# The second and third mixer of a three-layer fp32 network on one core: where the operands of the first output rows and the recurrence stand in the queues

## The chip, the cores and the metric

The kernel runs on one core of a Trainium2 chip. The core has TensorE (PE, the matrix engine, with its weight loads shown apart as PEld), VectorE (DVE), ScalarE (ACT), GpSimd (POOL) and SyncE (SP, here the queue that loads weights). Each engine works through its own queue in order, and the engines wait for one another on semaphores. The metric is the device time of the kernel in microseconds (us), the median of several runs. 0.2% of it is 1.9 us.

## What is computed

A sequence of 256 tokens (with 16 meta tokens ahead of it in the first layer) and a model width of 1024, all in fp32. A first layer with three kinds of mixing and a gated MLP, then two layers of which each has a mixer and a squared-ReLU MLP. The change touches only the mixers of these two layers:

```python
def mixer_ab(h, w_in, conv_w, ln_g, ln_b, w_out):        # "second mixer"
    u = h @ w_in
    u_val, u_gate, q, k, v = jnp.split(u, ...)
    ya = conformer_conv(u_val, u_gate, conv_w, ln_g, ln_b)   # GLU, 31 taps, layer norm, silu
    yb = moba_attention(q, k, v)                             # 8 heads of 64, causal, ALiBi
    return jnp.concatenate([ya, yb], axis=-1) @ w_out

def mixer_c(h, w_in, conv_w, conv_b, w_r, b_r, w_i, b_i, lam, w_out):   # "third mixer"
    gate, xr = jnp.split(h @ w_in, 2, axis=-1)
    xr = causal_depthwise_conv(xr, conv_w) + conv_b          # 4 taps
    r, i = sigmoid(xr @ w_r + b_r), sigmoid(xr @ w_i + b_i)
    a = exp(-8 * r * softplus(-lam))
    hseq = scan(a, sqrt(1 - a * a) * (i * xr))               # h_t = a_t h_{t-1} + b_t
    return (hseq * gelu(gate)) @ w_out
```

## The kernel before

**Weights and splitting.** All weights come as 275 slabs of 128x1024, in the order of use, through a ring of four buffers (`raw`, `whi`, `wlo`). To keep fp32 accuracy each slab is split in two parts: ACT copies it rounded to `whi` (L428), DVE subtracts to get `wlo` (L801). Activations are split in the same way, into `ahi` (ACT) and `alo` (DVE), or `hidhi` and `hidlo` for the hidden units of the MLPs. A product is then three matmuls, L1168 to L1170. `split_ahead(n)` splits slab n + 3 while slab n is used, since the buffer of slab n + 3 was that of slab n - 1.

**Columns and rows.** A "column" multiplies one slab of an input projection with all eight chunks of the activations, 24 matmuls, and DVE takes the result out of its bank with `take` (L843) into `proj`. Column i may start when `take` has emptied the bank of column i - 2. A "row" of an output projection multiplies chunk k of the mixed values with its slab into four banks that hold the whole output, again 24 matmuls. Its operand is prepared by `operand_hi` (ACT, L474) and then `operand_lo` (DVE, L817), both out of `af[:, k]`. Since `ahi` and `alo` hold the operand of the columns too, ACT waits for the last column (`slab_used`) before it writes the first row's part into `ahi`.

**What sets the order.** The order is written out by hand in each engine's program. In the second mixer one loop of slots u = 0 to 18 runs on every engine: attention of head pair s = u // 2 (scores, maxima, exponentials L495, normalizing L868, transposes, copies L517, values L1280), beside it the remaining columns (`IN2_STEP`, the last at u = 11), the parts of the convolution and its layer norm (L1055 multiplies by the inverse deviation), and the first rows (`OUT2_STEP`: row 0 at u = 13, row 1 at 14, row 2 at 16, row 3 at 17). `CAT2_STEP` says in which slot the operands of these rows are made: operand 0 at u = 12, operand 1 at 13.

**Third mixer.** Sixteen columns, first the eight of the recurrent branch (i = 0 to 7), then the eight of the gate branch (i = 8 to 15). Beside them DVE does the four taps (L1125), ACT the sigmoids and, at i = 10, eight exponentials (L757); POOL multiplies `y` by `af` (L397, eight) and squares the decay (L400, eight, each after its exponential); `decay_steps` (DVE, L1106, eight) multiplies (a² + 1) by a hyperbolic tangent, which gives a² - 1, in one instruction with both inputs in SBUF; ACT takes two square roots of four chunks each (L762); `recur(j)` multiplies (L1113) and scans (L1114); `gated_output(j)` multiplies by the GELU (L1137); then the operand is split and row j can run.

## Time and profile before

| | |
|---|---|
| runs | 954.03 us median of three (953.94 to 955.48) |
| profiled execution | 954.74 us, of it 953.0 us span |
| PE busy | 911.9 us (96% of the span) |
| DVE, ACT, POOL busy | 591.7, 464.6, 92.4 us |
| mean granted TensorE clock | 0.984 of full |

TensorE is busy nearly all the time, and the chain of work that ended last lies on it for 87% of the span. So a change of order can gain only where TensorE stands idle or runs at its lower clock. A line of a timeline gives start and length in us, engine and line, and in brackets how long the engine was idle before it and what ended the idle time.

### The profile page before, as it was taken

The numbers are of one execution on the slowest core, as the hardware profiler recorded it, in microseconds if no ns is written. First come the engines' busy times: TensorE is split into PE (matmuls) and PEld (weight loads), VectorE is DVE, ScalarE is ACT, GpSimd is POOL, SyncE is SP. The second block draws the span as 40 slices with busy tenths as digits, with TensorE's granted clock in tenths as the row PEclk, the third lists the DMA queues.
The fourth block names the chain that finished last, engine by engine and source line by source line (L and its number), as shares of the span: only waits on it lengthen the run. The fifth ranks groups of instructions, "written<-read, shape, count | busy, mean of one in ns | idle before, by whom it ended". The sixth has DMA issues, their size and how long they took to land.

```text
span 953.0 us, 19688 instructions
## 1 busy us (share of the span) xinstructions
PE 911.9 (96%) x7466; PEld 874.3 (92%) x7466; DVE 591.7 (62%) x962; ACT 464.6 (49%) x733; POOL 92.4 (10%) x153
## 2 busy tenths in 40 slices
PE   7999898999999999999899999999898999999996
PEld 7988688999999998977899999999898999999995
DVE  4666345666656576545476656666878865666555
ACT  5444455534444355433664444444777654444442
POOL 4110000200000004910010000000221100000001
PEclk8999799999999999999999999999999999999998
DMA  6433122655555653732435555555334455555541
GB/s 229 161 128 125 53 67 90 221 188 187 180 179 192 196 185 124 238 107 76 160 129 191 192 185 193 177 183 193 132 134 155 155 173 188 190 177 185 189 154 45
DMA packets 44079, 152.57 MB, mean 160 GB/s; under 512 B 5764, under 2 KB 6020, under 8 KB 44036
## 3 DMA queue, kind: packets, MB, share of 16 engines
q1 hardware_dynamic: 40752, 146.36, 46.5%
q0 software_dynamic: 2912, 5.48, 1.8%
q8 instruction: 30, 0.49, 0.2%
q10 hardware_dynamic: 372, 0.14, 0.1%
q14 instruction: 13, 0.11, 0.0%
HBM read 148.58 MB, written 1.05 MB: 157 GB/s over the span
## 4 chain that ended last, share of the span: by engine, by line
PE 87%; DVE 7%; ACT 4%; issue 1%; DMA 1%; SPq 0%; DVEq 0%; ACTq 0%
PE bank L1168 25%; PE bank L1170 25%; PE bank L1169 25%; DVE alo L824 2%; PE bank L1454 2%; PE bank L1381 2%; DVE h L834 1%; DVE wlo L801 1%; PE bank L1237 1%; ACT whi L428 1%; PE bank L1197 1%; PE bank L1536 1%; PE bank L1254 1%; DMA raw<-in_slabs 1%; PE bank L1190 1%
## 5 line engine op out<-in xcount | busy, mean ns | idle before, releaser
L1168 PE MATMUL bank<-ahi,whi 128*128 128x256 f32 (+1 forms) x1416 | 407.1, 288 | 11.0 <-DVE alo L817 5.8
L1170 PE MATMUL bank<-ahi,wlo 128*128 128x256 f32 (+1 forms) x1416 | 400.9, 283 | 0.0
L1169 PE MATMUL bank<-alo,whi 128*128 128x256 f32 (+1 forms) x1416 | 400.6, 283 | 0.0
L801 DVE TENSOR_TENSOR wlo<-raw,whi 128x1024 fp32r<-128x1024 f32 x275 | 336.5, 1232 | 40.7 <-ACT whi L428 40.4
L428 ACT ACTIVATE whi<-raw 128x1024 fp32r<-128x1024 f32 x275 | 284.5, 1051 | 129.6 <-PE bank L1170 119.0
L1168 PEld LDWEIGHTS bank<-ahi,whi 128*128 128x128 f32 x1416 | 269.7, 190 | 14.6 <-DVE alo L817 6.8
L1169 PEld LDWEIGHTS bank<-alo,whi 128*128 128x128 f32 x1416 | 269.7, 190 | 0.4
L1170 PEld LDWEIGHTS bank<-ahi,wlo 128*128 128x128 f32 x1416 | 269.9, 191 | 0.0
L1168 PE MATMUL bank<-hidhi,whi 128*128 128x256 f32 x688 | 192.8, 280 | 0.0
L1169 PE MATMUL bank<-hidlo,whi 128*128 128x256 f32 x688 | 192.5, 280 | 0.0
L1170 PE MATMUL bank<-hidhi,wlo 128*128 128x256 f32 x688 | 192.5, 280 | 0.0
L1169 PEld LDWEIGHTS bank<-hidlo,whi 128*128 128x128 f32 x688 | 129.5, 188 | 0.0
L1168 PEld LDWEIGHTS bank<-hidhi,whi 128*128 128x128 f32 x688 | 129.4, 188 | 0.0
L1170 PEld LDWEIGHTS bank<-hidhi,wlo 128*128 128x128 f32 x688 | 129.4, 188 | 0.0
L1067 DVE SCALAR_TENSOR_TENSOR hid<-bank,rstd 128x256 f32<-128x256 f32 x64 | 27.1, 424 | 126.5 <-PE bank L1170 124.4
L710 ACT ACTIVATE hidhi<-hid 128x256 fp32r<-128x256 f32 x64 | 26.9, 420 | 137.1 <-DVE hid L1067 133.9
L843 DVE SCALAR_TENSOR_TENSOR proj<-bank,rstd 128x256 f32<-128x256 f32 (+1 forms) x56 | 23.8, 427 | 61.1 <-PE bank L1170 58.8
L332 POOL TENSOR_TENSOR sq<-sq 128x256 f32<-128x256 f32 (+1 forms) x20 | 19.7, 1013 | 355.0 <-ACT sq L456 355.0
L621 ACT ACTIVATE hidhi<-hid 128x256 fp32r<-128x256 f32 x22 | 9.2, 418 | 61.9 <-DVE hid L991 61.9
L1190 PE MATMUL bank<-ahi,whi 128*128 128x256 f32 (+1 forms) x96 | 25.8, 306 | 8.4 <-ACT ahi L449 4.3
L387 POOL DMA_DIRECT2D shared<-zpad x64 | 31.4, 499 | 1.2 <-POOL zpad L382 1.2
L1074 DVE TENSOR_TENSOR hidlo<-hid,hidhi 128x256 fp32r<-128x256 f32 x64 | 27.2, 425 | 3.5 <-ACT hidhi L710 1.1
(183 smaller groups left out, 720.4 us busy)
## 6 DMA issues: line engine op xcount, KB each, us to landing
raw<-in_slabs SPq DMA_DIRECT2D x275, 512.0 KB, 3.4
shared<-zpad POOLq DMA_DIRECT2D x64, 35.5 KB, 3.1
shared<-in_convw POOLq DMA_DIRECT2D x4, 512.0 KB, 6.3
h<-in_xT SPq DMA_DIRECT2D x4, 272.0 KB, 4.0
vtok<-in_gatew POOLq DMA_DIRECT2D x2, 512.0 KB, 4.9
out<-y SPq DMA_DIRECT2D x4, 256.0 KB, 2.2
par<-in_par ACTq DMA_DIRECT2D x1, 72.0 KB, 3.2
poolw<-in_poolw ACTq DMA_DIRECT2D x1, 64.0 KB
```

Of the source, the lines that this page charges most:

```text
L332: pool.tensor_tensor(t8[:, j, :] if i == N_MIX0 else a, a, b, ALU.add).then_inc(sum_ready, 1)
L387: pool.dma_start(zsh[32 * s:32 * s + 32, k, g, :], zpad[32 * g:32 * g + 32, k, s:s + CONV_X])\
L428: act.activation(whi[:, n % R, :, :], raw[:, n % R, :, :], ACT.Copy).then_inc(hi_done, 1)
L710: act.activation(hidhi[:, f % 2, :], hid[:, f % 2, :], ACT.Square).then_inc(hid_hi, 1)
L801: dve.tensor_tensor(wlo[:, n % R, :, :], raw[:, n % R, :, :], whi[:, n % R, :, :].bitcast(F32), ALU.subtract).then_inc(lo_done, 1)
L843: dve.scalar_tensor_tensor(proj[:, d, lo:], src[:, lo:T1], scale, rstd[:, lo:], ALU.mult, ALU.mult).then_inc(gemm_evac, 1)
L1067: dve.scalar_tensor_tensor(hid[:, f % 2, :], col_bank(f)[:, NMETA:T1], 0.0, rstd[:, NMETA:], ALU.max, ALU.mult).then_inc(gemm_evac, 1)
L1074: dve.tensor_tensor(hidlo[:, f % 2, :], hid2[:, f % 2, :], hidhi[:, f % 2, :].bitcast(F32), ALU.subtract).then_inc(hid_lo, 1)
L1168: pe.matmul(dst, hi, xh, start=start, stop=False, skip_group_check=True)
L1169: pe.matmul(dst, hi, xl, start=False, stop=False, skip_group_check=True)
L1170: return pe.matmul(dst, lo, xh, start=False, stop=stop, skip_group_check=True)
L1190: pe.matmul(dst, w[:, slot, k, :], ahi[:, k, lo:], start=(k == 0 and w is whi), stop=False, skip_group_check=True)
```

## The change

In the second mixer (slots u):

- DVE: the layer norm's four multiplications (L1055) go ahead of the `take` of slot 11. Operand 0 follows this `take`, ahead of the slab split and of slot 12's maxima.
- ACT: the wait for the last column and `operand_hi` of operand 0 come first in slot 12, ahead of slot 12's probability copies and exponentials. The copy of the transposed values (`vtok`) stands ahead of the exponentials in slots 0, 4, 8 and 12, no longer behind them.
- PE: row 0 also waits for the `vtok` copy of the last head pair.

In the third mixer:

- The operands of rows 0 and 1 go to `hidhi` and `hidlo`, so ACT's wait for the last column moves from operand 0 to operand 2.
- `decay_steps` moves a column sooner: the first four stand between the `take` of i = 10 and its slab split, the others behind i = 11. The square roots, `recur(0)` and the GELUs move a column sooner too, and `recur(1)` now stands inside the column loop.
- Behind the columns, `operand_lo(j)` stands ahead of `gated_output(j + 1)`.

The diff:

```diff
@@ -279,6 +279,12 @@
...
+        def row_operand(s, k):
+
+            if s == A_LRU and k < 2:
+                return hidhi[:, k, :], hidlo[:, k, :]
+            return ahi[:, k, NMETA:], alo[:, k, NMETA:]
+
         def half(b, j):
@@ -471,7 +477,7 @@
...
                 act.wait_ge(af_ready, KC * f + k + 1)
-                act.activation(ahi[:, k, NMETA:], af[:, k, :], ACT.Copy).then_inc(ahi_ready, 1)
+                act.activation(row_operand(s, k)[0], af[:, k, :], ACT.Copy).then_inc(ahi_ready, 1)
@@ -652,22 +658,23 @@
...
                     n += 1
+                if u == max(IN2_STEP) + 1:
+                    act.wait_ge(slab_used, OUT2)
+                    operand_hi(A_CAT2, F_CAT2, CAT2_STEP[u])
                 if u % 2 == 0:
...
                         transposed(u // 2 - 1, FOX_S, moba_copies)
+                    if u % 4 == 0 and u < MOBA_U:
+                        pair = u // 4
+                        act.wait_ge(vT, 7 + pair)
+                        act.activation(vtok[:, 0:2, P * pair:P * pair + P],
+                                       acc_bank[2][:, 0:2 * P].rearrange("p (g d) -> p g d", g=2), ACT.Copy).then_inc(v_ready, 1)
                     if u // 2 < MOBA_S:
                         probabilities(u // 2, FOX_S, MOBA_N)
-                if u % 4 == 0 and u < MOBA_U:
-                    pair = u // 4
-                    act.wait_ge(vT, 7 + pair)
-                    act.activation(vtok[:, 0:2, P * pair:P * pair + P],
-                                   acc_bank[2][:, 0:2 * P].rearrange("p (g d) -> p g d", g=2), ACT.Copy).then_inc(v_ready, 1)
                 if u >= 6 and u % 4 == 2:
...
                     act.activation(af[:, PAIR_CHUNK[pair], :], aux_bank[:, 0:SEQ], ACT.Copy).then_inc(af_ready, 1)
-                if u == max(IN2_STEP) + 1:
-                    act.wait_ge(slab_used, OUT2)
                 if 2 <= u <= 2 * CONV_C and u % 2 == 0:
@@ -685,7 +692,7 @@
...
                             .then_inc(af_ready, 1)
-                if u in CAT2_STEP:
+                if u in CAT2_STEP and u > max(IN2_STEP) + 1:
                     operand_hi(A_CAT2, F_CAT2, CAT2_STEP[u])
@@ -756,19 +763,18 @@
...
                            .then_inc(lru_exp, 1)
-                if i in (12, 13):
-                    j = 4 * (i - 12)
+                if i in (11, 12):
+                    j = 4 * (i - 11)
                     act.wait_ge(lru_m2, j + 4)
...
                        .then_inc(lru_root, 4)
-                if i == 14:
-                    gelus(0, 3)
-            act.wait_ge(slab_used, OUT3)
+                if i in (13, 14):
+                    gelus(3 * (i - 13), 3 * (i - 12))
             for j in range(KC):
+                if j == 2:
+                    act.wait_ge(slab_used, OUT3)
                 operand_hi(A_LRU, F_LRU, j)
                 split_ahead(OUT3 + j - 1)
-                if j == 0:
-                    gelus(3, 6)
                 if j == 1:
@@ -814,8 +820,8 @@
...
                 dve.wait_ge(ahi_ready, KC * s + k + 1)
-                dve.tensor_tensor(alo[:, k, NMETA:], af[:, k, :], ahi[:, k, NMETA:].bitcast(F32), ALU.subtract)\
-                   .then_inc(alo_ready, 1)
+                hi, lo = row_operand(s, k)
+                dve.tensor_tensor(lo, af[:, k, :], hi.bitcast(F32), ALU.subtract).then_inc(alo_ready, 1)
@@ -1034,25 +1040,28 @@
...
+                if u == max(IN2_STEP) + 1:
+                    operand_lo(A_CAT2, CAT2_STEP[u])
+                    split_ahead(OUT2 - 1)
                 softmax_slot(u, MOBA_S, FOX_S, MOBA_N, alibi_bias)
+                if u == LN_VAR_STEP + 1:
+                    dve.wait_ge(ln_std, 1)
+                    for k in range(CONV_C):
+                        dve.tensor_tensor(cv[:, k, :], cv[:, k, :], r1[:, :], ALU.mult).then_inc(ln_norm, 1)
                 if u in IN2_STEP:
                     c = IN2_STEP[u]
-                    take(n, acc_bank[n % 2], c, QSCALE if 8 <= c < 12 else 1.0)
+                    take(n, acc_bank[n % 2], c, QSCALE if 8 <= c < 12 else 1.0, ahead=n < OUT2 - 1)
                     n += 1
...
                     n += 1
-                if u in CAT2_STEP:
+                if u in CAT2_STEP and u > max(IN2_STEP) + 1:
                     operand_lo(A_CAT2, CAT2_STEP[u])
...
                                                  ALU.mult, ALU.add).then_inc(ln_dev, 1)
-                if u == LN_VAR_STEP + 1:
-                    dve.wait_ge(ln_std, 1)
-                    for k in range(CONV_C):
-                        dve.tensor_tensor(cv[:, k, :], cv[:, k, :], r1[:, :], ALU.mult).then_inc(ln_norm, 1)
             for i in range(max(CAT2_STEP.values()) + 1, KC):
@@ -1114,7 +1123,10 @@
...
             for i, c in enumerate(IN3_ORDER):
-                take(IN3 + i, col_bank(i), c, ahead=IN3 + i < OUT3 - 1)
+                take(IN3 + i, col_bank(i), c, ahead=IN3 + i < OUT3 - 1 and i != 10)
+                if i == 10:
+                    decay_steps(range(4))
+                    split_ahead(IN3 + i)
                 if 1 <= i <= KC:
@@ -1127,20 +1139,19 @@
...
                     ins.then_inc(af_ready, 1)
-                if i in (11, 12):
-                    decay_steps(range(4 * (i - 11), 4 * (i - 10)))
-                if i == 13:
-                    recur(0)
+                if i == 11:
+                    decay_steps(range(4, KC))
+                if i in (12, 13):
+                    recur(i - 12)
...
             gated_output(0)
-            recur(1)
             for j in range(KC):
+                operand_lo(A_LRU, j)
                 if j + 1 < KC:
                     gated_output(j + 1)
-                operand_lo(A_LRU, j)
                 split_ahead(OUT3 + j - 1)
@@ -1210,7 +1221,7 @@
...
                 pe.wait_ge(alo_ready, KC * s + i + 1)
-                row(n0 + i, ahi[:, i, NMETA:], alo[:, i, NMETA:], first=(i == 0), last=(i == KC - 1))
+                row(n0 + i, *row_operand(s, i), first=(i == 0), last=(i == KC - 1))
@@ -1480,6 +1491,8 @@
...
                 if u in OUT2_STEP:
+                    if OUT2_STEP[u] == 0:
+                        pe.wait_ge(v_ready, 10)
                     operand_row(OUT2, A_CAT2, OUT2_STEP[u])
```

The changed kernel has the same number of instructions on each engine; in it a line number is 6 to 12 higher than before. First DVE's queue in the second mixer, slots 11 and 12: `proj` is the `take` of the last column, `t` the layer norm, `ssb` and `nmax` the maxima, `alo` operand 0. Before:

```order
L843 SCALAR_TENSOR_TENSOR proj<-bank,rstd 128x256 [waits slab_used]
L801 TENSOR_TENSOR wlo<-raw,whi 128x1024 [waits hi_done]
L1055 TENSOR_TENSOR t<-t,r 128x256 [waits ln_std]
L1055 TENSOR_TENSOR t<-t,r 128x256 x3
L1032 SCALAR_TENSOR_TENSOR ssb<-dist,bank 128x128 [waits p_ready,s_ready]
L1032 SCALAR_TENSOR_TENSOR ssb<-dist,bank 128x128 [waits p_ready]
L859 TENSOR_REDUCE nmax<-ssb 128x1 [waits s_biased] x2
L817 TENSOR_TENSOR alo<-af,ahi 128x256 [waits ahi_ready]
```

Now:

```order
L1050 TENSOR_TENSOR t<-t,r 128x256 [waits ln_std]
L1050 TENSOR_TENSOR t<-t,r 128x256 x3
L849 SCALAR_TENSOR_TENSOR proj<-bank,rstd 128x256 [waits slab_used]
L824 TENSOR_TENSOR alo<-af,ahi 128x256 [waits ahi_ready]
L807 TENSOR_TENSOR wlo<-raw,whi 128x1024 [waits hi_done]
L1038 SCALAR_TENSOR_TENSOR ssb<-dist,bank 128x128 [waits p_ready,s_ready]
L1038 SCALAR_TENSOR_TENSOR ssb<-dist,bank 128x128 [waits p_ready]
L865 TENSOR_REDUCE nmax<-ssb 128x1 [waits s_biased] x2
```

The layer norm went from behind the last `take` to ahead of it, and `alo` from behind the maxima to right behind the `take`, ahead of the slab split `wlo`.

ACT's queue at the same place, slot 12: `prob` are the exponentials, `probT` and `vtok` the copies out of the banks, `ahi` operand 0. Before:

```order
L428 ACTIVATE whi<-raw 128x1024 [waits slab_used,raw_loaded1]
L517 ACTIVATE probT<-bank 128x2x256 [waits o_ready,pT]
L495 ACTIVATE prob,rsum<-ssb,nmax 128x128 [waits pT,m_ready] x2
L663 ACTIVATE vtok<-bank 128x2x128 [waits vT]
L474 ACTIVATE ahi<-af 128x256 [waits af_ready,slab_used]
L428 ACTIVATE whi<-raw 128x1024 [waits slab_used,raw_loaded2]
```

Now:

```order
L434 ACTIVATE whi<-raw 128x1024 [waits slab_used,raw_loaded1]
L480 ACTIVATE ahi<-af 128x256 [waits af_ready,slab_used]
L523 ACTIVATE probT<-bank 128x2x256 [waits o_ready,pT]
L670 ACTIVATE vtok<-bank 128x2x128 [waits vT]
L501 ACTIVATE prob,rsum<-ssb,nmax 128x128 [waits pT,m_ready] x2
L434 ACTIVATE whi<-raw 128x1024 [waits slab_used,raw_loaded2]
```

`ahi`, with its wait for the last column, went from behind the exponentials to the head of the slot, and `vtok` ahead of the exponentials.

Last DVE's queue in the third mixer, from the `take` of i = 10 on: `sq<-sq,t` are the decay steps, `y` and `t` the two instructions of `recur`. Before:

```order
L843 SCALAR_TENSOR_TENSOR proj<-bank,rstd 128x256 [waits slab_used]
L801 TENSOR_TENSOR wlo<-raw,whi 128x1024 [waits hi_done]
L843 SCALAR_TENSOR_TENSOR proj<-bank,rstd 128x256 [waits slab_used]
L801 TENSOR_TENSOR wlo<-raw,whi 128x1024 [waits hi_done]
L1106 SCALAR_TENSOR_TENSOR sq<-sq,t 128x256 [waits lru_aa] x4
L843 SCALAR_TENSOR_TENSOR proj<-bank,rstd 128x256 [waits slab_used]
L801 TENSOR_TENSOR wlo<-raw,whi 128x1024 [waits hi_done]
L1106 SCALAR_TENSOR_TENSOR sq<-sq,t 128x256 [waits lru_aa] x4
L843 SCALAR_TENSOR_TENSOR proj<-bank,rstd 128x256 [waits slab_used]
L801 TENSOR_TENSOR wlo<-raw,whi 128x1024 [waits hi_done]
L1113 TENSOR_TENSOR y<-y,sq 128x256 [waits lru_ix,lru_root]
L1114 SCALAR_TENSOR_TENSOR t<-proj,y 128x256 [waits dve_chain]
```

Now:

```order
L849 SCALAR_TENSOR_TENSOR proj<-bank,rstd 128x256 [waits slab_used]
L1115 SCALAR_TENSOR_TENSOR sq<-sq,t 128x256 [waits lru_aa] x4
L807 TENSOR_TENSOR wlo<-raw,whi 128x1024 [waits hi_done]
L849 SCALAR_TENSOR_TENSOR proj<-bank,rstd 128x256 [waits slab_used]
L807 TENSOR_TENSOR wlo<-raw,whi 128x1024 [waits hi_done]
L1115 SCALAR_TENSOR_TENSOR sq<-sq,t 128x256 [waits lru_aa] x4
L849 SCALAR_TENSOR_TENSOR proj<-bank,rstd 128x256 [waits slab_used]
L807 TENSOR_TENSOR wlo<-raw,whi 128x1024 [waits hi_done]
L1122 TENSOR_TENSOR y<-y,sq 128x256 [waits lru_ix,lru_root]
L1123 SCALAR_TENSOR_TENSOR t<-proj,y 128x256 [waits dve_chain]
L849 SCALAR_TENSOR_TENSOR proj<-bank,rstd 128x256 [waits slab_used,dve_chain]
L807 TENSOR_TENSOR wlo<-raw,whi 128x1024 [waits hi_done]
```

The first four decay steps stand ahead of the split and of the next `take`, the second four ahead of the `take` of i = 12, and `recur(0)` ahead of the `take` of i = 13.

## Rows read from the trace of the kernel before

**Rows 1.** Waits of TensorE, 440 to 485: us in total, times, longest.

```profile
PE bank L1168 <- DVE alo L817: 4.7, 2, 3.2
```

**Rows 2.** Timeline of TensorE, second mixer: start us, us, instruction, idle before.

```profile
450.72 0.66 PE L1280 MATMUL bank<-probT,vtok 128*64 128x128 f32 x8 [0.47 <-ACT probT L517]
454.55 0.39 PE L1168 MATMUL bank<-ahi,whi 128*128 128x256 f32 x1 [3.17 <-DVE alo L817]
...
459.10 0.70 PE L1254 MATMUL bank<-proj 64*128 64x256 f32 x4
...
459.93 0.37 PE L1168 MATMUL bank<-ahi,whi 128*128 128x256 f32 x1
...
462.96 0.44 PE L1280 MATMUL bank<-probT,vtok 128*64 128x128 f32 x4
```

**Rows 3.** TensorE by stretches: window, length, busy, granted clock, DMA share, GB/s.

```profile
455.60:459.00 3.40, 3.40 (x18) 0.50 0.44 146
469.00:483.00 14.00, 14.00 (x115) 1.00 0.63 219
730.60:755.20 24.60, 24.52 (x192) 0.93 0.53 172
```

**Rows 4.** Timeline of DVE, second mixer.

```profile
449.07 0.42 DVE L843 SCALAR_TENSOR_TENSOR proj<-bank,rstd 128x256 f32<-128x256 f32 x1 [2.85 <-PE bank L1170]
449.41 1.22 DVE L801 TENSOR_TENSOR wlo<-raw,whi 128x1024 fp32r<-128x1024 f32 x1
450.54 1.42 DVE L1055 TENSOR_TENSOR t<-t,r 128x256 f32<-128x256 f32 x4
451.88 0.48 DVE L1032 SCALAR_TENSOR_TENSOR ssb<-dist,bank 128x128 f32<-128x128 f32 x2
...
454.07 0.43 DVE L817 TENSOR_TENSOR alo<-af,ahi 128x256 fp32r<-128x256 f32 x1 [1.32 <-ACT ahi L474]
```

**Rows 5.** Timeline of ACT, second mixer.

```profile
452.59 0.40 ACT L495 ACTIVATE prob<-ssb,nmax 128x128 f32<-128x128 f32 x1 [1.92 <-DVE nmax L859]
...
453.64 0.40 ACT L474 ACTIVATE ahi<-af 128x256 fp32r<-128x256 f32 x1
```

**Rows 6.** Timeline of TensorE, third mixer: column 14, then output row 0.

```profile
721.10 0.39 PE L1168 MATMUL bank<-ahi,whi 128*128 128x256 f32 x1 [0.21 <-DVE proj L843]
...
730.63 0.36 PE L1168 MATMUL bank<-ahi,whi 128*128 128x256 f32 x1 [3.65 <-issue]
```

**Rows 7.** Line L400 on POOL: duration ns min/median/max, first and last start.

```profile
L400 POOL TENSOR_TENSOR sq<-proj x8: 607/607/1592, 713.7 to 717.8; 128x256 f32<-128x256 f32 x8
```

**Rows 8.** Line L1125 on DVE, one in three beside POOL: the same columns.

```profile
L1125 DVE SCALAR_TENSOR_TENSOR af<-proj,par,af x24: 479/485/900, 680.7 to 707.9; 128x256 f32<-128x256 f32 x24
```

**Rows 9.** Timeline of DVE and POOL side by side, behind the third mixer.

```profile
757.26 4.70 DVE L824 SCALAR_TENSOR_TENSOR alo<-h,par,ahi 128x256 fp32r<-128x256 f32 x8
...
758.97 3.59 POOL L332 TENSOR_TENSOR sq<-sq 128x256 f32<-128x256 f32 x4 [39.54 <-ACT sq L456]
```

**Rows 10.** Timeline of DVE, third mixer.

```profile
722.10 1.42 DVE L1106 SCALAR_TENSOR_TENSOR sq<-sq,t 128x256 f32<-128x256 f32 x4
...
726.79 1.22 DVE L801 TENSOR_TENSOR wlo<-raw,whi 128x1024 fp32r<-128x1024 f32 x1
727.92 0.42 DVE L843 SCALAR_TENSOR_TENSOR proj<-bank,rstd 128x256 f32<-128x256 f32 x1
...
728.59 0.42 DVE L1113 TENSOR_TENSOR y<-y,sq 128x256 f32<-128x256 f32 x1
...
729.77 0.42 DVE L1137 TENSOR_TENSOR af<-t,proj 128x256 f32<-128x256 f32 x1
730.11 0.42 DVE L817 TENSOR_TENSOR alo<-af,ahi 128x256 fp32r<-128x256 f32 x1
```

**Rows 11.** Timeline of ACT, third mixer: a table load, and the first operand.

```profile
720.79 1.28 ACT L762 ACT_TABLE_LOAD   x1 [2.48 <-DVE sq L1106]
...
728.76 0.42 ACT L474 ACTIVATE ahi<-af 128x256 fp32r<-128x256 f32 x1 [0.62 <-DVE af L1137]
```

## The prediction

> **What bounds the kernel.** TensorE is busy for 96% of the span, so I first looked for where it waits, in the list of waits: in the second mixer it waits twice for an operand of an output row, 4.7 us together, the longer 3.2 [rows 1]. The timeline puts the longer one ahead of output row 0: the value products of slot 13 begin at 450.72 and last 0.66, then nothing until 454.55 [rows 2]. The granted clock then falls to 0.50 (1.2 GHz) from 455.6 to 459.0 [rows 3]; row 0 with what follows it takes 459.10 - 454.55 = 4.55, row 1 at full clock 462.96 - 459.93 = 3.03 [rows 2]. So the pause costs 3.17 and the fall 1.52. Behind the second wait, 4.7 - 3.17 = 1.5 long, the clock is 1.00 [rows 1, 3]. The third mixer has the same picture: TensorE stands for 3.65 ahead of row 0 (730.63) [rows 6], and the eight rows behind run at a mean clock of 0.93 over 24.6 us [rows 3], which costs 0.07 x 24.6 = 1.7. Together these are 3.17 + 1.52 + 3.65 + 1.7 = 10.0 us; the question is how much of them the new order can take away.
>
> **Second mixer.** Operand 0 is late because ACT makes it behind the exponentials (452.59), and these wait for the maxima, which DVE makes behind the split (449.41) and four layer norm multiplications (450.54 to 451.88) [rows 4, 5]. None of that is needed for it. Now: the last column is done at 449.07, when its `take` begins. ACT stands idle there and makes `ahi` in 0.40 [rows 5], done at 449.5; `take` needs 0.34 of DVE (449.07 to 449.41), then `alo` needs 0.43 [rows 4], done at 449.95. TensorE is still busy with its attention work until 450.72 + 0.66 = 451.38 [rows 2]. Row 0 also waits for the `vtok` copy, which is now behind the probability copy that releases the values at 450.72 [rows 2]; a copy of 0.4 as on line L474 [rows 5] ends at 451.1, hidden. So row 0 starts at 451.35 and the pause of 3.17 goes whole.
>
> What is late next? The multiplications fit into DVE's 2.85 of idle time ahead of the `take` (1.34 needed) [rows 4]. The split starts at 449.9 and the maxima at 449.9 + 1.13 = 451.0, against 451.88: 0.85 sooner. The exponentials are then at 451.75, and all that follows up to operand 1 moves with them: ACT's two exponentials 0.8, slab split 1.0, operand 0.4 give 453.8; DVE's slab split (1.13) starts at 453.5, operand 1 is ready at 455.05. TensorE comes to row 1 at 451.35 + 3.03 = 454.4, plus scores and transposes 0.83 (459.10 to 459.93) [rows 2] = 455.2. That is just enough. Row 1 starts 459.93 - 455.15 = 4.8 sooner if the clock no longer falls. Row 2 and the table load with the four Silu that cause the second wait follow TensorE's transposes and move by the same amount; that wait of 1.5 stays. The earlier `vtok` copies in slots 0, 4, 8 delay exponentials by 0.3 at most, ahead of a normalization that stands behind a column of TensorE: nothing. **Sum of the second mixer: -4.7**, with -3.1 if the clock falls all the same, and nothing beyond -4.8.
>
> **Third mixer.** Here I follow DVE, which decides. Before, the decay steps stood where POOL's squares were done. POOL makes the eight squares from 713.7 on, one each 0.58 ((717.8 - 713.7)/7), though the last took 1.59 [rows 7]. Now DVE comes to the first step after the `take` at 712.8 and has to wait for them, with the split of slab 13 and the `take` of column 11 queued behind it, on which TensorE's column 13 waits.
>
> And the two engines disturb one another. L1125, also an instruction with both inputs in SBUF, takes 0.48 alone and 0.90 where POOL multiplies beside it [rows 8]. Behind the third mixer POOL's four sums and L824 run in turns: four sums take 3.59, one each 0.87 = 0.57 + 0.30 [rows 9]. I take that turn for the decay steps. The Trainium skill, "SBUF — State Buffer", section "Who interferes with whom", says that a VectorE instruction with two SBUF inputs and a GpSimd instruction that reads SBUF exclude one another for a whole instruction. By that rule the decay steps beside POOL's squares run in turns, as the rows show for L1125 and L824; the case without it is a rival below.
>
> The steps, in us: square 0 is done at 714.3, but square 1 has begun, so step 0 runs behind it and is done at 715.1; steps 1 to 3 each 0.87 later, 717.7. A square goes first (718.3), then the split of slab 13: 719.4. `take` of column 11 done at 719.75. TensorE was ready for column 13 at 721.10 - 0.21 - 2.84 = 718.05 [rows 6] and starts at 719.8: a **new wait of 1.75**. DVE: split of slab 14, behind a square, 721.0; last square 721.6; four more steps 721.6 to 722.9 (1.42 alone, less the 0.08 by which an end overlaps the next start [rows 10]); `take` 12 done 723.25; column 14 could start at 722.65, starts at 723.3: wait 0.6. Then split 1.13, `recur(0)` 1.18 (728.59 to 729.77), `take` 0.34, split 1.13, `recur(1)` 1.18, `take` 0.34, split 1.13 [rows 10]: DVE reaches the last `take` at 729.55, column 15 was done at 728.95. `take` and `gated_output(0)` 0.67 (727.92 to 728.59) and 0.1 to finish: 730.3; ACT's `ahi` 0.42 [rows 11], hop, DVE's 0.42 [rows 10]: row 0 at **731.3**, against 730.63, after a wait of 2.35. ACT keeps up: its table load of 1.28 [rows 11] and roots begin at 717.8, and its last split is done at 728.1, DVE needs it at 728.4. The place in `hidhi` gains nothing by itself, since `gated_output(0)` still stands behind the last `take`.
>
> Behind it the order `operand_lo(j)`, `gated_output(j + 1)`, split, `recur` has the same sum as before, 0.34 + 0.34 + 1.13 + 1.18 = 3.0 for a row of 2.84. Operand 1 is ready 3.25 after operand 0, row 6 starts at 731.3 + 3.25 + 5 x 3.0 = 749.5, row 7 at 752.35, its end is 755.2: as before (755.15), if the clock stays up, because row 0 alone is later while the fall of 1.7 is spared. If it falls again (2.35 lies between 1.5 without and 3.17 with a fall [rows 1, 2]), DVE's slower pace hides a part: end 755.7. I take the middle. **Sum of the third mixer: +0.3** (0 to +0.6).
>
> **Total:** -4.7 + 0.3 = -4.4. The profiled execution took 954.74, which gives 950.3; the median of the runs is 0.7 lower, so the forecast is 954.03 - 4.4 = **949.6**.
>
> **Rivals.** (a) No turns between DVE and POOL: the four steps end at 716.4, slab 13 at 717.6, the `take` in time for 718.05; no new wait, row 0 at 728.9, rows paced by DVE end at 752.75 to 753.2, that is -2.1. Time 954.03 - 4.7 - 2.1 = 947.2. Against it speak rows 8 and 9; for it, that the decay step was never seen beside more than one square. (b) The clock falls in the second mixer all the same, since its attention work leaves TensorE short pauses (0.47 ahead of the values [rows 2]): 949.6 + 1.6 = 951.2. (c) Slower than before: POOL keeps the read path for all eight squares. At 0.87 each they end at 713.7 + 7.0 = 720.7, the four steps at 722.0, slab 13 at 723.2, column 13 starts at 723.6, 5.6 late. That pause is longer than both that brought a fall; against the forecast it costs 2.5 on DVE's path and two falls of 1.7 more, 5.9: 949.6 + 5.9 = 955.5. It decides from a start of column 13 some 3 us behind 719.8 on. (d) The moved operand does not release row 0, because another semaphore comes last (the slab, the bank of `vtok`): nothing is gained in the second mixer, 954.3. Against it: both lie ahead of 451.35 by the times above.
>
> **Numbers.** Forecast 0.62, (a) 0.15, (b) 0.15, (c) 0.03, (d) 0.05. The range takes in (a) and (b) with the spread of the runs: 946.8 to 951.9. 0.2% is 1.9 us, about what a measurement can tell: faster (below 952.1) 0.92, same 0.06, slower 0.02.
>
> **What would show it.** Second mixer: no wait of TensorE for `alo` ahead of row 0, clock 1.00 through rows 0 and 1, operand 1 within 0.2 of TensorE's arrival, and the wait ahead of row 3 still near 1.5. Third: squares and decay steps in turns at 0.87, a wait of 1.5 to 2 ahead of column 13, row 0 behind a pause of 2.3. I am wrong if column 13 starts without a wait (then 947), or if row 1 waits for its operand by more than 1 us.

## The result, and the profile after

The changed kernel takes **949.27 us** (median of 6 runs, 946.81 to 950.37); the kernel before took 955.01 beside it (6 runs, 953.94 to 955.48). The ratio is 0.9941, with a 95% interval of 0.9925 to 0.9957; the medians differ by 5.7 us. The forecast was 949.6, or 4.4 faster than the 954.03 shown with the kernel before.

The head of the profile's page after the change (busy time and instructions of each engine, then the granted clock in 40 slices, in tenths):

```profile
span 945.1 us, 19688 instructions
PE 907.3 (96%) x7466; PEld 869.1 (92%) x7466; DVE 593.4 (63%) x962; ACT 464.2 (49%) x733; POOL 93.7 (10%) x153
PEclk9999899999999999999999999999999999999998
```

The instruction counts are those of before. POOL is busy for 1.3 us more, though it does the same squares: a first sign of what the third mixer does now. TensorE's waits for output operands in the second mixer (440 to 480; us in total, times, longest):

```profile
PE bank L1179 <- DVE alo L824: 1.5, 1, 1.5
```

and in the third mixer (695 to 760), the first two rows:

```profile
PE bank L1179 <- issue: 2.1, 1, 2.1
PE bank L1179 <- DVE proj L849: 1.5, 2, 1.3
```

Of the two waits for `alo` in [rows 1], 4.7 together, the longer one is gone and the one of 1.5 stands. In the third mixer the pause ahead of row 0 has shrunk from 3.65 [rows 6] to 2.1 ("issue": the trace names nothing that ended the wait; DVE finishes operand 0 at 723.11, 0.1 ahead of row 0, so it is most likely the operand), and there is a new wait of 1.3 for the `take` of column 11, ahead of column 13. The wait of 0.2 ahead of column 14 was there before [rows 6]. The same stretches by engine (length, busy us of PE, PEld, DVE, ACT, POOL, the granted clock, DMA share, GB/s):

```profile
448.00:459.40 11.40, 11.38 (x96) 10.28 (x98) 8.11 (x20) 9.17 (x20) 0.00 (x0) 1.00 0.44 146
710.00:723.20 13.20, 9.60 (x77) 9.00 (x77) 12.58 (x21) 10.05 (x11) 3.49 (x3) 1.00 0.52 166
723.20:747.80 24.60, 23.88 (x192) 22.92 (x193) 22.77 (x39) 13.40 (x20) 0.00 (x0) 1.00 0.54 189
```

Through rows 0 to 2 of the second mixer TensorE works without a gap at full clock (11.38 of 11.40), where [rows 3] has a clock of 0.50 for 3.40 us. In the third mixer the clock also stays at 1.00, where [rows 3] has a mean of 0.93.

**Where the time went.** The profiled execution took 946.81, which is 7.9 less than the 954.74 of before. To divide this, I took the starts of the same matmuls in both traces and compared the lengths between them:

| stretch (time in the kernel before) | after less before, us | forecast |
|---|---|---|
| start to the first MLP (to 178.66) | -2.67 | 0 |
| from there to the last column of slot 11 (445.93) | -0.03 | 0 |
| second mixer's end: slot 11 to MLP 2 (484.47) | **-4.81** | -4.7 |
| MLP 2 to the first gate product (682.42) | -0.03 | 0 |
| third mixer: from there to MLP 3 (755.71) | **-0.37** | +0.3 |
| MLP 3 to the end | -0.02 | 0 |

The first row is no work of the change: the code up to there is the same. The second row shows that the earlier `vtok` copies of slots 0, 4 and 8 cost nothing. Two stretches of the first row in the trace of before (columns as above):

```profile
5.00:25.00 20.00, 15.94 (x103) 15.44 (x102) 10.42 (x15) 11.49 (x18) 12.04 (x21) 0.83 0.68 240
105.00:125.00 20.00, 17.88 (x90) 15.94 (x90) 9.05 (x16) 9.05 (x17) 0.00 (x0) 0.74 0.08 26
```

and after:

```profile
5.00:25.00 20.00, 16.08 (x112) 15.58 (x111) 11.24 (x16) 12.29 (x20) 11.77 (x21) 0.91 0.70 257
105.00:125.00 20.00, 18.85 (x104) 16.82 (x104) 8.12 (x15) 9.38 (x19) 0.00 (x0) 0.83 0.15 53
```

The granted clock is higher in both, over nearly the same work: by 0.08 and 0.09 of 20 us, which is 1.6 and 1.8 us of full clock, enough for the 2.67. So 4.81 + 0.37 = 5.2 us belong to the change, and 2.7 to how this one execution met the clock. All comparisons below go by such lengths, beside the medians.

### The profile page after: what moved, and what is told of

Its sections match the earlier page's. It is cut to its first block, busy times and chain, and to the rows that moved or that the text cites. A ratio compares the mean times of both kernels' runs of the same rounds, so it can differ in the third digit from the quotient of the medians.

```text
span 945.1 us, 19688 instructions
## 1 busy us (share of the span) xinstructions
PE 907.3 (96%) x7466; PEld 869.1 (92%) x7466; DVE 593.4 (63%) x962; ACT 464.2 (49%) x733; POOL 93.7 (10%) x153
## 4 chain that ended last, share of the span: by engine, by line
PE 86%; DVE 8%; ACT 3%; issue 1%; DMA 1%; SPq 0%; DVEq 0%; POOL 0%; ACTq 0%
PE bank L1179 25%; PE bank L1181 25%; PE bank L1180 25%; DVE alo L830 2%; PE bank L1465 2%; DVE wlo L807 2%; PE bank L1392 1%; DVE h L840 1%; PE bank L1248 1%; ACT whi L434 1%; PE bank L1208 1%; PE bank L1265 1%; PE bank L1279 1%; PE bank L1549 1%; PE bank L1291 1%
## 5 line engine op out<-in xcount | busy, mean ns | idle before, releaser
L1179 PE MATMUL bank<-ahi,whi 128*128 128x256 f32 (+1 forms) x1400 | 401.3, 287 | 5.6 <-DVE proj L849 2.8
L1181 PE MATMUL bank<-ahi,wlo 128*128 128x256 f32 (+1 forms) x1400 | 394.4, 282 | 0.0
L1180 PE MATMUL bank<-alo,whi 128*128 128x256 f32 (+1 forms) x1400 | 394.3, 282 | 0.0
L1179 PEld LDWEIGHTS bank<-ahi,whi 128*128 128x128 f32 x1400 | 264.9, 189 | 9.8 <-DVE alo L824 3.9
L1180 PEld LDWEIGHTS bank<-alo,whi 128*128 128x128 f32 x1400 | 265.0, 189 | 0.4
L1181 PEld LDWEIGHTS bank<-ahi,wlo 128*128 128x128 f32 x1400 | 265.2, 189 | 0.0
L1179 PE MATMUL bank<-hidhi,whi 128*128 128x256 f32 x704 | 197.3, 280 | 2.3 <-issue 2.1
L1180 PE MATMUL bank<-hidlo,whi 128*128 128x256 f32 x704 | 196.9, 280 | 0.0
L1181 PE MATMUL bank<-hidhi,wlo 128*128 128x256 f32 x704 | 196.8, 280 | 0.0
L1179 PEld LDWEIGHTS bank<-hidhi,whi 128*128 128x128 f32 x704 | 132.4, 188 | 2.7 <-issue 2.3
L1201 PE MATMUL bank<-ahi,whi 128*128 128x256 f32 (+1 forms) x96 | 24.7, 297 | 8.2 <-ACT ahi L455 4.2
```

What stands on the lines that cost most here:

```text
L1179: pe.matmul(dst, hi, xh, start=start, stop=False, skip_group_check=True)
L1180: pe.matmul(dst, hi, xl, start=False, stop=False, skip_group_check=True)
L1181: return pe.matmul(dst, lo, xh, start=False, stop=stop, skip_group_check=True)
L1201: pe.matmul(dst, w[:, slot, k, :], ahi[:, k, lo:], start=(k == 0 and w is whi), stop=False, skip_group_check=True)
```

## The experiments

Every experiment is a variant of the changed kernel. First, all stage lengths in one table, against the kernel before; "fall" says whether the granted clock falls to half for a stretch of the third mixer.

| kernel | second mixer | third mixer | fall | median, us (runs) | ratio to before, 95% |
|---|---|---|---|---|---|
| after | -4.81 | -0.37 | no | 949.27 (6) | 0.9941, 0.9925 to 0.9957 |
| e1_second_only | -4.75 | +0.02 | yes | 947.99 (7) | 0.9942, 0.9921 to 0.9963 |
| e2_third_only | -0.02 | -0.01 | yes | 954.23 (12) | 0.9995, 0.9978 to 1.0011 |
| e3_decay_psum | -4.83 | -1.55 | yes | 943.62 (1) | |
| e4_operand0_early | -4.75 | -0.72 | no | 949.50 (8) | 0.9945, 0.9924 to 0.9967 |
| e5_tanh_psum | -4.72 | -1.54 | yes | 948.36 (6) | 0.9928, 0.9906 to 0.9949 |
| e6_silu_early | -6.37 | -0.10 | yes | 947.72 (6) | 0.9927, 0.9906 to 0.9949 |
| e7_all | -6.38 | -2.37 | no | 946.15 (6) | 0.9903, 0.9882 to 0.9925 |
| e8_decay_half_later | -4.87 | -0.38 | yes | 950.11 (1) | |
| e9_norm_behind | -3.41 | -0.25 | no | 948.54 (1) | |
| e10_operands_in_ahi | -4.83 | +0.14 | yes | 951.50 (1) | |

The ratio is that of the comparison in which the kernel was run, with its own runs of before beside it; it is not the quotient of two medians. For e7 the medians are 946.15 and 954.39, which alone would give 0.9914, and for e1 947.99 and 954.86, which would give 0.9928.

Each stage length comes from one execution, so "fall" says what that one execution met. Single runs say little by their time (e3 met a good clock in the first layer, e10 a bad one, as shown at the end); their stage lengths are what counts.

### e1_second_only and e2_third_only: one half of the change each

e1 takes the third mixer back to what it was, e2 the second. The core of e1:

```
             for i, c in enumerate(IN3_ORDER):
-                take(IN3 + i, col_bank(i), c, ahead=IN3 + i < OUT3 - 1 and i != 10)
-                if i == 10:
-                    decay_steps(range(4))
-                    split_ahead(IN3 + i)
+                take(IN3 + i, col_bank(i), c, ahead=IN3 + i < OUT3 - 1)
...
-                if i == 11:
-                    decay_steps(range(4, KC))
+                if i in (11, 12):
+                    decay_steps(range(4 * (i - 11), 4 * (i - 10)))
```

The core of e2:

```
-                if u == max(IN2_STEP) + 1:
-                    operand_lo(A_CAT2, CAT2_STEP[u])
-                    split_ahead(OUT2 - 1)
                 softmax_slot(u, MOBA_S, FOX_S, MOBA_N, alibi_bias)
```

> Only the second mixer's part of the change; the third mixer is as before. My theory: this part removes the pause of 3.17 us ahead of row 0 and the fall of the clock behind it, 4.7 to 4.8 us from the layer norm's variance product to row 3, and the wait of 1.5 ahead of row 3 stays. Against the kernel before: 4 to 5 us faster, ratio 0.995 to 0.996. In the third mixer the pause of 3.6 ahead of row 0 and its fall of the clock are there as before. Rival (the clock falls in the second mixer all the same): 3.1 us faster, ratio 0.997.

> Only the third mixer's part of the change; the second mixer is as before. The trace of the changed kernel shows this stage 0.4 us shorter than before, with a new wait of 1.3 ahead of column 13, and without a fall of the clock. My theory: the part is worth 0 to 0.5 us, ratio 0.9995 to 1.000. Rival: the 1.3 us by which the medians differ more than the forecast (5.7 against 4.4) come from here; then it is 1.0 to 1.7 us faster, ratio 0.998 to 0.999. A third reading: they come from the clock in the first layer, outside both mixers; then neither this kernel nor the one with the second part alone shows them as a steady gain.

e1 has the whole gain of the second mixer (-4.75), and its ratio, 0.9942, lies just below the 0.995 to 0.996 that was expected; its third mixer has the pause of 3.6 and the fall, as before. e2 has no gain in the second mixer: there the clock falls at 454.1 as before. The part in the third mixer is worth nothing that can be measured: ratio 0.9995 (0.9978 to 1.0011) with 12 runs, and -0.01 by the stage, with a fall in it. (Without a fall, as in the profiled execution after the change, the same third mixer gives 0.37.) So the measurable gain is the second mixer's, and rival (d), that another semaphore holds row 0, is out.

### e9_norm_behind: is operand 1 just in time?

The forecast gave row 1 its operand 0.15 ahead of TensorE, thanks to the layer norm multiplications that no longer stand ahead of the maxima. Here they stand there again; all else is as in the changed kernel.

```
+                if u == max(IN2_STEP) + 1:
                     dve.wait_ge(ln_std, 1)
                     for k in range(CONV_C):
                         dve.tensor_tensor(cv[:, k, :], cv[:, k, :], r1[:, :], ALU.mult).then_inc(ln_norm, 1)
+                softmax_slot(u, MOBA_S, FOX_S, MOBA_N, alibi_bias)
```

> The changed kernel, with the layer norm's four multiplications put back behind the take of the last column, ahead of slot 12's maxima; operand 0 stays early. Theory (operand 1 was ready only just in time, as the forecast said): the pause ahead of row 0 stays gone, the maxima and all behind them come 1.3 us later, row 1 waits 1.2 to 1.4 us for its operand, and the second mixer is 3.4 to 3.6 us shorter than before instead of 4.8. Rival (only operand 0's place counts): 4.8 as in the changed kernel.

DVE in the changed kernel (start, us, operation; in brackets the idle time before it and what ended it):

```profile
446.82 0.43 DVE L824 TENSOR_TENSOR alo<-af,ahi 128x256 fp32r<-128x256 f32 x1
...
448.30 0.48 DVE L1038 SCALAR_TENSOR_TENSOR ssb<-dist,bank 128x128 f32<-128x128 f32 x2
452.01 0.42 DVE L824 TENSOR_TENSOR alo<-af,ahi 128x256 fp32r<-128x256 f32 x1
```

TensorE there, first matmuls of row 0 and row 1:

```profile
448.61 0.38 PE L1179 MATMUL bank<-ahi,whi 128*128 128x256 f32 x1
452.48 0.39 PE L1179 MATMUL bank<-ahi,whi 128*128 128x256 f32 x1
```

DVE in e9:

```profile
448.54 1.43 DVE L1049 TENSOR_TENSOR t<-t,r 128x256 f32<-128x256 f32 x4
449.88 0.48 DVE L1038 SCALAR_TENSOR_TENSOR ssb<-dist,bank 128x128 f32<-128x128 f32 x2
453.60 0.42 DVE L824 TENSOR_TENSOR alo<-af,ahi 128x256 fp32r<-128x256 f32 x1
```

TensorE in e9, row 1:

```profile
454.07 0.39 PE L1179 MATMUL bank<-ahi,whi 128*128 128x256 f32 x1 [1.12 <-DVE alo L824]
```

In the changed kernel operand 0 is ready at 447.25, 1.35 ahead of row 0, and operand 1 at 452.43, 0.05 ahead of row 1: just in time indeed. In e9 the 1.34 of multiplications push the chain back, TensorE waits 1.12 at row 1 (just under the 1.2 to 1.4 expected), and the stage gives 3.41 instead of 4.81. Row 1 starts 1.34 later than in the changed kernel, counted from slot 11, and 1.12 of this is that wait. The clock does not fall behind it. So the move of the layer norm is worth 1.4, somewhat over a quarter of the gain. What the new place of slot 12's `vtok` copy does by itself was not tried.

### e6_silu_early: the wait of 1.5 that was left

The table load of the four Silu and the Silu themselves stand ahead of the operand of row 3. In e6 the load comes with the first Silu a slot sooner, and the slab splits go behind the operands that are due.

```
-                if u == MOBA_U:
-                    for k in range(CONV_C):
...
+                if u == MOBA_U - 1:
+                    silu(0)
+                if u == MOBA_U:
+                    silu(1)
+                    split_ahead(n)
+                    silu(2)
+                    silu(3)
+                    n += 1
```

> The changed kernel, with ACT's table load and first Silu of the convolution branch in slot 15, ahead of the last probability copies, and operands 3 and 4 ahead of the slab splits. Theory (the wait of 1.5 us ahead of row 3 comes from the table load and four Silu behind the last probability copy, as the forecast said): the wait goes, the second mixer is 1.4 to 1.5 us shorter than in the changed kernel, no fall of the clock. Rival (another semaphore comes just behind, the slab or operand 4): under 0.7 us, with a wait ahead of row 4 or 5.

ACT in the changed kernel:

```profile
455.69 1.06 ACT L434 ACTIVATE whi<-raw 128x1024 fp32r<-128x1024 f32 x1 [0.39 <-PE bank L1181]
...
457.25 1.28 ACT L693 ACT_TABLE_LOAD   x1
458.55 2.08 ACT L693 ACTIVATE af<-t,par 128x256 f32<-128x256 f32 x4
460.53 0.40 ACT L480 ACTIVATE ahi<-af 128x256 fp32r<-128x256 f32 x1
```

ACT in e6 (this execution runs 2.1 later at this place, from the first layer):

```profile
457.44 1.28 ACT L660 ACT_TABLE_LOAD   x1
458.74 0.60 ACT L660 ACTIVATE af<-t,par 128x256 f32<-128x256 f32 x1
459.25 0.58 ACT L523 ACTIVATE probT<-bank 128x512 f32<-128x512 f32 x1
459.72 0.41 ACT L480 ACTIVATE ahi<-af 128x256 fp32r<-128x256 f32 x1
```

The load starts 1.9 sooner (457.44 - 2.1 against 457.25), where the changed kernel has a short idle time and a slab split; the last probability copy comes 0.5 later for it (459.25 - 2.1 against 456.65 in the changed kernel). TensorE's list of waits for this stretch has no wait for `alo` any more. The stage is 1.56 shorter still: the wait of 1.5 was all on the path. No fall came behind it in the second mixer; the one in the table is in the third, whose code is that of the changed kernel.

### e3_decay_psum and e5_tanh_psum: do DVE and POOL take turns?

The forecast said that a decay step, both of whose inputs lie in SBUF, runs in turns with POOL's squares. Both experiments leave the order and change where one of the two inputs lies. e3 reads some bank of PSUM in its place, with a minimum for the product, so its values are not those of the network. e5 keeps what is computed: ACT's Tanh writes its result to PSUM.

```
-                    dve.scalar_tensor_tensor(sq[:, j, NMETA:], sq[:, j, NMETA:], 1.0, t8[:, j, :], ALU.add, ALU.mult)\
+                    dve.scalar_tensor_tensor(sq[:, j, NMETA:], sq[:, j, NMETA:], 1.0, tanh_place(j), ALU.add, ALU.mult)\
                        .then_inc(lru_m2, 1)
...
-                act.activation(t8[:, k, :], sq[:, k, NMETA:], ACT.Tanh, scale=lam[:, 3, k:k + 1])
+                act.activation(tanh_place(k), sq[:, k, NMETA:], ACT.Tanh, scale=lam[:, 3, k:k + 1])
```

The edit of e3 is this line in place of the decay step:

```
+                    dve.scalar_tensor_tensor(sq[:, j, NMETA:], sq[:, j, NMETA:], -1.0, half(aux_bank, 0), ALU.mult, ALU.min)\
```

> The changed kernel, with the decay steps' second input taken from a PSUM bank (and a minimum with a negated square in place of the product), so that each reads SBUF once; its values are not the reference's. Theory (DVE and POOL exclude one another while both read SBUF): the first four steps fall from 3.08 us to 1.8 to 2.0 (they still wait for the squares at 0.57 each), POOL's eight squares from 7.3 to under 5.5 us, column 13 waits under 0.3 us instead of 1.3. Rival (the steps are slow because they wait for the squares one by one, whatever they read): the first four steps stay at 3 us and column 13 waits over 1 us.

> The changed kernel, with the hyperbolic tangents that the decay steps read written to free PSUM banks by ACT, so that a decay step reads SBUF once; the result is the reference's. Theory (DVE and POOL exclude one another, and DVE's sum of work up to operand 7 sets the end of the third mixer): the first four steps take 2.1 us instead of 3.08, column 13 waits under 0.3, and the third mixer ends 1.1 to 1.9 us sooner than in the changed kernel (0.4 less than before there), that is 1.5 to 2.3 less than before. Rival (POOL's squares are merely pushed against DVE's splits, and row 7 comes no sooner): under 0.5 us sooner than the changed kernel.

DVE in the changed kernel, from the first decay step on (the first line is four steps in one; the second and third are two of them by themselves):

```profile
706.83 3.08 DVE L1115 SCALAR_TENSOR_TENSOR sq<-sq,t 128x256 f32<-128x256 f32 x4 [1.47 <-POOL sq L406]
707.57 0.83 DVE L1115 SCALAR_TENSOR_TENSOR sq<-sq,t 128x256 f32<-128x256 f32 x1
708.32 0.83 DVE L1115 SCALAR_TENSOR_TENSOR sq<-sq,t 128x256 f32<-128x256 f32 x1
...
709.83 1.63 DVE L807 TENSOR_TENSOR wlo<-raw,whi 128x1024 fp32r<-128x1024 f32 x1
711.39 0.41 DVE L849 SCALAR_TENSOR_TENSOR proj<-bank,rstd 128x256 f32<-128x256 f32 x1
...
713.69 0.41 DVE L1115 SCALAR_TENSOR_TENSOR sq<-sq,t 128x256 f32<-128x256 f32 x1
```

POOL there, the eight squares in one and two of them by themselves:

```profile
706.18 7.31 POOL L406 TENSOR_TENSOR sq<-proj 128x256 f32<-128x256 f32 x8 [2.43 <-ACT proj L764]
708.08 0.79 POOL L406 TENSOR_TENSOR sq<-proj 128x256 f32<-128x256 f32 x1
708.84 0.79 POOL L406 TENSOR_TENSOR sq<-proj 128x256 f32<-128x256 f32 x1
```

TensorE there, column 13 and row 0:

```profile
711.85 0.39 PE L1179 MATMUL bank<-ahi,whi 128*128 128x256 f32 x1 [1.27 <-DVE proj L849]
723.21 0.36 PE L1179 MATMUL bank<-hidhi,whi 128*128 128x256 f32 x1 [2.14 <-issue]
```

DVE in e5:

```profile
707.76 0.42 DVE L1120 SCALAR_TENSOR_TENSOR sq<-sq,bank 128x256 f32<-128x256 f32 x1 [1.51 <-POOL sq L411]
708.34 0.42 DVE L1120 SCALAR_TENSOR_TENSOR sq<-sq,bank 128x256 f32<-128x256 f32 x1 [0.15 <-POOL sq L411]
708.91 0.42 DVE L1120 SCALAR_TENSOR_TENSOR sq<-sq,bank 128x256 f32<-128x256 f32 x1
709.49 0.42 DVE L1120 SCALAR_TENSOR_TENSOR sq<-sq,bank 128x256 f32<-128x256 f32 x1 [0.15 <-POOL sq L411]
709.82 1.28 DVE L812 TENSOR_TENSOR wlo<-raw,whi 128x1024 fp32r<-128x1024 f32 x1
711.03 0.41 DVE L854 SCALAR_TENSOR_TENSOR proj<-bank,rstd 128x256 f32<-128x256 f32 x1
```

With both inputs in SBUF four steps take 3.08. They start 0.75 apart, three distances and a last step of 0.83 making the 3.08, and POOL's squares start 0.75 apart too, each between two steps: the two engines take turns. Where no square is left a step takes 0.41 and the next starts 0.34 behind it (713.69, 714.03). With one input in PSUM four steps take 709.49 + 0.42 - 707.76 = 2.15, one each 0.57 to 0.58, which is POOL's own pace: DVE now only waits 0.15 for the next square. The split behind them takes 1.28 instead of 1.63. In sum the `take` of column 11 ends 3.68 after the first step instead of 4.97, and TensorE's list of waits for this kernel has no wait ahead of column 13. e3 shows the same: four steps in 2.13, its stage -1.55 against -1.54.

The Trainium skill, "SBUF — State Buffer", section "Who interferes with whom", says that a VectorE instruction with two SBUF inputs contends with a GpSimd instruction that reads SBUF, under an exclusive lock. This case agrees that they hold each other up, and only when both inputs are in SBUF: 0.75 for a step and a square, against 0.57. It does not show the two simply one after the other, which would take 0.57 + 0.34 = 0.91.

Two expectations failed in e3: the four steps were to take 1.8 to 2.0, and took 2.13, and POOL's eight squares were to take under 5.5, and took 6.58 (7.31 in the changed kernel). The splits, with both inputs in SBUF, still stand against the squares, so neither experiment shows the stage without any turns.

### e8_decay_half_later: is the wait ahead of column 13 lost time?

```
-                if i == 10:
-                    decay_steps(range(4))
+                if i in (11, 12):
+                    decay_steps(range(4 * (i - 11), 4 * (i - 10)))
                     split_ahead(IN3 + i)
...
-                if i == 11:
-                    decay_steps(range(4, KC))
```

> The changed kernel, with the four decay steps half a column later: behind the take of column 11 and ahead of the split of slab 14, and behind the take of column 12 and ahead of the split of slab 15. Theory (the wait of 1.3 us ahead of column 13 comes from the slab split and the take that queue behind the decay steps, and costs nothing at the end, since DVE's work sets it): column 13 does not wait, there is a wait of 0.5 to 1.5 ahead of column 15 instead, and the stage ends within 0.6 us of the changed kernel's, clock falls aside. Rival (the wait ahead of column 13 is lost time): the stage ends 1.0 to 1.5 us sooner.

The waits of TensorE in e8's third mixer, first two rows:

```profile
PE bank L1177 <- issue: 2.3, 1, 2.3
PE bank L1177 <- DVE proj L849: 1.2, 1, 1.2
```

Column 13 starts without a wait, but the wait reappears with 1.2 ahead of column 15, and the stage is as long as in the changed kernel (-0.38 and -0.37), though e8 has a fall in it. So the wait ahead of column 13 was not 1.3 of lost time. But the order is worth something: against e2 and e6, which have a fall and the changed kernel's third mixer (-0.01 and -0.10), e8 is 0.3 to 0.4 better. DVE's operation for operand 0 starts 0.40 sooner (47.41 behind the first gate product, against 47.81 in the changed kernel), with one step fewer beside a square. For the rest DVE has more work in this stretch than TensorE (12.58 busy of 13.20 against 9.60, in the window from 710 above), so its sum decides: where TensorE waits for it is mostly a matter of place.

### e10_operands_in_ahi and e4_operand0_early: the place and the time of operand 0

e10 puts the first two operands of the third mixer back into `ahi` and `alo`.

```
             for j in range(KC):
-                if j == 2:
+                if j == 0:
                     act.wait_ge(slab_used, OUT3)
```

> The changed kernel, with the operands of the third mixer's rows 0 and 1 in ahi and alo again, and ACT's wait for the last column ahead of operand 0. Theory (gated_output(0) stands behind the last take, so the place in hidhi gains nothing by itself): row 0 starts within 0.1 us of where it does in the changed kernel, counted from the stage's first gate product. Rival: 0.4 us or more later, since ACT is held.

Counted from the first gate product, row 0 starts 0.18 later than before in e10 and 0.13 later in the changed kernel: the place gains nothing by itself, as forecast, because `gated_output(0)` still stands behind the last `take`. (The +0.14 at its stage's end has a fall in it; e2 and e6 have one too and stand at -0.01 and -0.10, so 0.15 to 0.24 in this one execution remain unexplained.) e4 uses the place: it moves `gated_output(0)` ahead of the last `take`, and operand 0 right behind it, ahead of its split.

```
+                if i == 13:
+                    gated_output(0)
+                if i == 14:
+                    operand_lo(A_LRU, 0)
+                    split_ahead(IN3 + i)
```

> The changed kernel, with gated_output(0) and operand 0 made ahead of the takes of the last two columns, which needs the place in hidhi. Theory (the place in hidhi gained nothing in the changed kernel, because gated_output(0) stands behind the last take): row 0 now waits 0.3 to 0.9 us instead of 2.1, and starts 1.4 to 1.8 sooner; behind it the rows go at DVE's pace of 3.0, so that of this 0.5 to 1.5 us is left at the end of the stage. 0.5 to 1.5 us faster than the changed kernel. Rival (DVE's pace takes it all back): row 7 starts no sooner, the time is that of the changed kernel within 0.3 us.

TensorE's waits in e4's third mixer:

```profile
PE bank L1188 <- DVE proj L852: 1.5, 2, 1.3
PE bank L1188 <- DVE hidlo L827: 1.3, 1, 1.3
...
PE bank L1188 <- issue: 0.5, 1, 0.5
```

DVE in e4, with operand 0 and operand 1:

```profile
722.56 0.43 DVE L827 TENSOR_TENSOR hidlo<-af,hidhi 128x256 fp32r<-128x256 f32 x1 [0.31 <-ACT hidhi L480]
727.02 0.42 DVE L827 TENSOR_TENSOR hidlo<-af,hidhi 128x256 fp32r<-128x256 f32 x1
730.01 0.42 DVE L827 TENSOR_TENSOR alo<-af,ahi 128x256 fp32r<-128x256 f32 x1
```

The pause ahead of row 0 falls from 2.1 to 0.5, and row 0 starts 1.65 sooner. But a new wait of 1.3 stands ahead of row 1, and only 0.35 is left at the end of the stage (-0.72 against -0.37); the main theory had expected 0.5 to 1.5. Operand 1 comes 4.46 after operand 0 here (727.02 - 722.56), and from then on one every 2.99: DVE's pace for a row, slower than TensorE's 2.84, sets the end. The two medians, 949.50 and 949.27, can't be told apart.

### e7_all: the version that gains most

e4, e5 and e6 together; the lines that stand for the three edits:

```
+                    operand_lo(A_LRU, 0)
+                act.activation(tanh_place(k), sq[:, k, NMETA:], ACT.Tanh, scale=lam[:, 3, k:k + 1])
+                if u == MOBA_U - 1:
+                    silu(0)
```

> Early Silu, tangents in PSUM, and operand 0 of the third mixer ahead of the last takes, together. Theory: the parts add up, 1.5 (second mixer) and 1.5 to 2.2 (third mixer) less than the changed kernel by the stages of the trace, 3.0 to 3.7 in all, against the kernel before 7.5 to 8.5 us: ratio 0.991 to 0.992. Rival (in the third mixer DVE's sum sets the end, so that the early operand 0 adds nothing to the tangents in PSUM): 2.6 to 3.0.

TensorE's waits in e7's third mixer, first row:

```profile
PE bank L1206 <- DVE hidlo L842: 1.4, 1, 1.4
```

The second mixer gives -6.38, as e6 does, and the third -2.37. That is 0.83 more than e5; e4's step alone was worth 0.35, the fall that e5 has and e7 has not is worth 0.1 to 0.4 (below), and up to 0.4 remains. An estimate accounts for it: e5's operation for operand 0 starts 1.57 sooner than in the changed kernel (46.24 behind the first gate product, against 47.81), so without a fall e5 would end at about -0.37 - 1.57 = -1.94; then its fall costs 0.40 and the early operand in e7 gives 0.43. Against the changed kernel the stages give 8.75 - 5.18 = 3.57, within the 3.0 to 3.7 expected, so the parts add up; the 8.75 itself is a little over the 7.5 to 8.5 expected against the kernel before. The median is 946.15, the ratio 0.9903 (0.9882 to 0.9925), where the stages say 8.75 of 954.4, or 0.9908. Its median is 8.2 us below before, and 3.1 below the changed kernel; these last two medians were taken in different comparisons, and the intervals of the two ratios just touch, so the second difference rests on the stages.

## Why the prediction was right, step by step

**Second mixer: -4.7 forecast, -4.81 measured.** Each step held. Operand 0 ready 1.4 ahead of TensorE: 1.35. No wait at row 0, clock at 1.00 through rows 0 and 1: so it is, and so the fall went with the pause that had come before it. Operand 1 within 0.2 of TensorE's arrival: 0.05, and e9 shows what hangs on it. The wait of 1.5 ahead of row 3 stays: 1.5, and e6 shows that it was real time. Rival (b), a fall all the same, came in none of the ten traces, one for each kernel that has this part of the change.

**Third mixer: +0.3 forecast (0 to +0.6), -0.37 measured.** The mechanism was right, its sizes too large.
- The turns: they came, but at 0.75 for a step and a square and not 0.87. The forecast took the 0.87 from another pair [rows 9], whose DVE instruction is a longer one (L824 takes 0.47 alone and 0.95 beside POOL, a decay step 0.41 and 0.83); that price did not carry over. The first step behaved as forecast: it starts at 706.83, beside square 1, and is done 1.5 after the first square's start (forecast 1.4). The fourth is done 3.7 after it (forecast 4.0), and the split behind takes 0.15 less than forecast. From the first square to the end of the `take` of column 11 the forecast had 6.05, and the trace has 711.80 - 706.18 = 5.62. The wait ahead of column 13 is therefore 1.3 and not 1.75, and the one ahead of column 14 is 0.2, as before, and not 0.6.
- This goes through to row 0: 0.13 later than before, forecast 0.7; its pause is 2.1, forecast 2.35.
- The rows behind: forecast no change at their end without a fall and +0.6 with one. Measured -0.37 and -0.25 without (after, e9), and -0.01 and -0.10 with one (e2, e6, which have the same third mixer). So about 0.4 of the 0.5 at row 0 stands here too, and the fall costs 0.15 to 0.36. The traces show why so little: without a fall (after) row 1 starts 3.22 behind row 0 and the next five rows 2.99 apart, which is DVE's pace; with one (e2) row 1 starts 4.43 behind row 0 and the rest 2.74 to 2.86 apart, which is TensorE's. At row 1 e2 is 1.20 later than the changed kernel, at row 7 only 0.35: TensorE makes up what it lost on rows that it would have waited for.
- The 1.7 that the forecast gave to the fall of before is a little large: the fall of the same length, 3.4 us, in the second mixer cost 1.52 [rows 2].
- Rival (a), no turns, fell by the pace of 0.75, and by e3 and e5, where it goes to 0.57. They also price the turns of the steps: -1.54 with a fall in it, against -0.37 without and -0.01 and -0.10 with one, so 1.2 to 1.5 us, where the forecast had 2.4 between its two cases, the turns of the splits included. POOL did not keep the read path (rival c): its squares and DVE's first four steps alternate.

**The total.** 5.2 by the stages, 5.7 by the medians, 4.4 forecast. The forecast errs by 0.7 in the third mixer and 0.1 in the second. The 0.5 between the stages and the medians lies within the spread of the runs; which part of it is more than chance is open. That 949.6 meets the median of 949.27 within 0.3 is in part luck: the change was worth 1.3 more by the medians than forecast, and the kernel before took 955.01 beside it, 1.0 more than the 954.03 from which the forecast started. The profiled execution alone would have said 7.9, and 2.7 of that have nothing to do with the change.

## What to carry to other kernels

An operand that a waiting TensorE needs next should stand in the queues ahead of work for later slots; ask for every instruction ahead of it whether something that is due soon hangs on it, and then what is late next (here the multiplications of a layer norm decided 1.4 of 4.8 us). Where VectorE works beside GpSimd, count the SBUF inputs of its instructions: moving one of two to PSUM was worth 1.2 to 1.5 us in the third mixer, more than any order of the queues tried there. Take the price of such turns from the same pair of instructions if a trace has it; another pair's was 0.12 a turn off. And where one engine has more work in a stretch than TensorE, reordering it mostly moves TensorE's wait from one column to the next.

## What the runs showed that was not expected

**The same code at another clock.** All kernels here have the same code in the first layer, and in the eleven profiled executions beside that of before the first MLP starts between 4.74 us sooner (e3) and 1.49 us later (e10) than there: a spread of 6.2 us. The granted clock shows it. e3 (columns as in the windows above):

```profile
5.00:25.00 20.00, 17.32 (x129) 16.82 (x128) 12.88 (x18) 14.18 (x22) 12.43 (x21) 1.00 0.74 258
105.00:125.00 20.00, 20.00 (x111) 17.45 (x111) 8.53 (x16) 9.94 (x18) 0.00 (x0) 0.83 0.16 53
```

e10:

```profile
105.00:125.00 20.00, 17.82 (x90) 15.82 (x90) 9.11 (x16) 9.12 (x17) 0.00 (x0) 0.74 0.08 26
```

That is as large as the spread of the 20 runs of before in the largest comparison (951.27 to 957.53), and larger than the change. What decides it in one execution was not found.

**Pauses of one length with and without a fall.** Ahead of row 0 of the third mixer TensorE stands for 2.1 to 2.3 in eight kernels: with no fall behind it after the change and in e9, with one in e2, e3, e5, e6, e8 and e10. The forecast left this open and took the middle. The runs leave it open too.

**A fall costs less than its length where another engine sets the pace.** In the second mixer of before it cost 1.52 [rows 2]; in the third, where DVE sets the pace, only 0.15 to 0.36 is to be seen between the four executions of the same third mixer (after, e9; e2, e6), where the forecast took 0.6.
